# One GpSimd copy of 4096 columns for each landed pair of weight units, in place of two of 2048, in a hybrid attention and mixture-of-experts block

## What is computed

```python
logits = (xt @ router_w + router_b)
top_v, top_e = lax.top_k(logits, TOP_K)          # 4 of 32 experts for each of 256 tokens
wts = jax.nn.softmax(top_v, axis=-1)
...
hgu = xb @ w_gate_up[e] + b_gate_up[e]           # 1024 x 2048 for each expert
gate, up = jnp.split(hgu, 2, axis=-1)
gate = jnp.minimum(gate, SWIGLU_LIMIT)
up = jnp.clip(up, -SWIGLU_LIMIT, SWIGLU_LIMIT)
act = (up + 1.0) * (gate * jax.nn.sigmoid(SWIGLU_ALPHA * gate))
return act @ w_down[e] + b_down[e]               # 1024 x 1024 for each expert
```

## Time and profile before

| what | us or share |
|---|---|
| median of three runs | 1407.03 |
| the profiled execution's own time | 1406.08 |
| its span, first to last instruction | 1404.4 |
| TensorE (PE) busy | 1348.0, 96% of the span |
| GpSimd (POOL) busy | 709.1, 50% |
| VectorE (DVE) busy | 399.0, 28% |
| ScalarE (ACT) busy | 236.9, 17% |
| landing transfers | 186 of 2048 KB, median 10.7 us from issue to landing |
| mean granted clock of TensorE | 0.988 of 2.4 GHz |

### The profile page before, as it was taken

How to read it: one execution, slowest core, us unless ns; L and a number is a source line. 1 busy time by engine, 2 the same in 40 slices (tenths; PEclk the granted TensorE clock), 3 DMA queues, 4 the chain that set the end, 5 groups by cost and what they waited for, 6 DMA issues and landing times.

```text
span 1404.4 us, 17038 instructions
## 1 busy us (share of the span) xinstructions
PE 1348.0 (96%) x6424; PEld 619.6 (44%) x6425; DVE 399.0 (28%) x751; ACT 236.9 (17%) x404; POOL 709.1 (50%) x413
## 2 busy tenths in 40 slices
PE   5999999999989999999999999999999999899996
PEld 2888445888643333333333333333333332233332
DVE  2150014565664213322232231123322211111112
ACT  2320024210022111111211211111211211111112
POOL 0000000000015427777587777777777777777774
PEclk9999999999979999999999999999999999999998
DMA  9743533599678658999799999999999999999995
GB/s 351 256 166 120 176 123 120 197 349 364 220 270 342 246 249 336 427 429 429 321 429 429 428 428 429 427 403 429 429 429 428 428 427 429 429 427 429 428 429 231
DMA packets 70913, 485.87 MB, mean 346 GB/s; under 512 B 7254, under 2 KB 7418, under 8 KB 45450
## 3 DMA queue, kind: packets, MB, share of 16 engines
q1 hardware_dynamic: 69490, 480.56, 83.5%
q0 software_dynamic: 1056, 3.93, 1.0%
q10 hardware_dynamic: 344, 1.07, 0.2%
HBM read 483.44 MB, written 2.10 MB: 346 GB/s over the span
## 4 chain that ended last, share of the span: by engine, by line
PE 50%; DMA 44%; POOL 1%; issue 1%; DVE 1%; SPq 1%; ACT 1%; POOLq 0%; DVEq 0%; ACTq 0%
DMA landing<-in_w_gate_up 29%; PE bank L1195 15%; DMA landing<-in_w_down 14%; PE bank L1531 12%; PE bank L1569 6%; PE bank L1204 6%; PE bank L1497 2%; PE bank L1430 2%; DMA piece<-in_w_ada 1%; PE bank L1545 1%; POOL dn_slot L503 1%; SPq L379 1%; PE bank L1559 0%; PE bank L1473 0%; PE bank L1409 0%
## 5 line engine op out<-in xcount | busy, mean ns | idle before, releaser
L503 POOL COPY gu_slot<-landing 128x2048 f32<-128x2048 f32 x248 | 462.9, 1896 | 208.3 <-issue 116.6
L1531 PE MATMUL bank<-gu_slot,xg 128*64 128x512 f32 x2304 | 518.8, 596 | 24.4 <-POOL gu_slot L503 24.2
L1531 PEld LDWEIGHTS bank<-gu_slot,xg 128*64 128x64 f32 x2304 | 159.5, 137 | 356.9 <-issue 273.4
L503 POOL COPY dn_slot<-landing 128x2048 f32<-128x2048 f32 x124 | 231.1, 1894 | 76.5 <-issue 56.5
L1569 PE MATMUL bank<-dn_slot,actT 128*64 128x512 f32 x1152 | 255.1, 595 | 0.0
L1569 PEld LDWEIGHTS bank<-dn_slot,actT 128*64 128x64 f32 x1152 | 79.5, 137 | 171.2 <-issue 171.2
L1195 PE MATMUL bank<-hT,piece 128*128 128x256 f32 x704 | 153.4, 380 | 0.0
L1126 DVE TENSOR_SCALAR bank<-bank 128x512 f32<-128x512 f32 x36 | 25.2, 700 | 417.7 <-PE bank L1531 417.7
L719 ACT ACTIVATE sig<-bank 128x512 f32<-128x512 f32 x36 | 21.5, 597 | 724.7 <-PE bank L1531 724.7
L1195 PEld LDWEIGHTS bank<-hT,piece 128*128 128x128 f32 x704 | 133.5, 190 | 19.0 <-issue 1.1
L1135 DVE TENSOR_TENSOR ysb<-bank,gt2q 128x512 f32<-128x512 f32 x36 | 24.9, 692 | 265.6 <-PE bank L1569 265.6
(11 more groups left out here) (292 smaller groups left out, 904.1 us busy)
## 6 DMA issues: line engine op xcount, KB each, us to landing
landing<-in_w_gate_up SPq DMA_DIRECT2D x124, 2048.0 KB, 10.7
landing<-in_w_down SPq DMA_DIRECT2D x62, 2048.0 KB, 10.7
piece<-in_w_in SPq DMA_DIRECT2D x17, 2048.0 KB, 8.6
piece<-in_w_ada SPq DMA_DIRECT2D x12, 2048.0 KB, 13.0
gu_slot<-in_w_gate_up SPq DMA_DIRECT2D x8, 1024.0 KB, 7.2
piece<-in_w_branch_a SPq DMA_DIRECT2D x2, 2048.0 KB, 9.2
dn_slot<-in_w_down SPq DMA_DIRECT2D x4, 1024.0 KB, 11.2
piece<-in_w_branch_b SPq DMA_DIRECT2D x2, 2048.0 KB, 8.5
```

Of the source, the lines that this page charges most:

```text
L503: nc.gpsimd.tensor_copy(place, landing[j // 2 % 3][:, j % 2, :]).then_inc(there, 16)
L1531: ins = M(gu_bank[u][64 * q:64 * q + 64, :], xg[:, k % 4, 64 * (k // 4):64 * (k // 4) + 64], gu_slot[k][:, cols_], start=(k == 0), stop=(k ...
```

## The change

Two units that lay side by side become one pair, with one tensor for both; gu_slot and dn_slot stay as views of its halves. GpSimd copies a landed block as one instruction of 4096 columns. It waits for the block's landing and for both units to have been used, and its end raises only the second unit's semaphore (gu_in or dn_in of 1, 3, 5, 7). TensorE waits once for each pair: for the second unit's semaphore at the value of the body's expert, and for the first unit's at 16, which the direct load of expert 0 brings it to. SyncE's waits stay as they are. VectorE's wait near the end is moved from gu_in[0] to gu_in[1].

```diff
-        gu_slot = [sb(f"gu_slot{j}", 8 * j, [P, 2048]) for j in range(8)]
-        dn_slot = [sb(f"dn_slot{j}", 64 + 8 * j, [P, 2, D]) for j in range(4)]
+        gu_pair = [sb(f"gu_pair{j}", 16 * j, [P, 4096]) for j in range(4)]
+        dn_pair = [sb(f"dn_pair{j}", 64 + 16 * j, [P, 4096]) for j in range(2)]
+        gu_slot = [gu_pair[j // 2][:, 2048 * (j % 2):2048 * (j % 2) + 2048] for j in range(8)]
+        dn_slot = [dn_pair[j // 2][:, 2048 * (j % 2):2048 * (j % 2) + 2048].rearrange("p (r n) -> p r n", r=2) for j in range(4)]
...
-                for j in range(12):
-                    place, there, used = ((gu_slot[j][:], gu_in[j], gu_used[j]) if j < 8 else
-                                          (dn_slot[j - 8][:].rearrange("p r n -> p (r n)"), dn_in[j - 8], (dn_used + [y_full])[j - 8]))
-                    pool.wait_ge(unit_landed[j // 2], 16 * e)
-                    pool.wait_ge(used, free)
-                    nc.gpsimd.tensor_copy(place, landing[j // 2 % 3][:, j % 2, :]).then_inc(there, 16)
+                for n in range(6):
+                    if n < 4:
+                        first, second, place, there = gu_used[2 * n], gu_used[2 * n + 1], gu_pair[n], gu_in[2 * n + 1]
+                    else:
+                        i = 2 * (n - 4)
+                        first, second, place, there = (dn_used + [y_full])[i], (dn_used + [y_full])[i + 1], dn_pair[n - 4], dn_in[i + 1]
+                    pool.wait_ge(unit_landed[n], 16 * e)
+                    pool.wait_ge(first, free)
+                    pool.wait_ge(second, free)
+                    nc.gpsimd.tensor_copy(place[:], landing[n % 3][:].rearrange("p a n -> p (a n)")).then_inc(there, 16)
...
-            dve.wait_ge(gu_in[0], 16 * E)
+            dve.wait_ge(gu_in[1], 16 * E)
...
-                    pe.wait_ge(gu_in[k], landed)
+                    if k % 2 == 0:
+                        pe.wait_ge(gu_in[k], 16)
+                        pe.wait_ge(gu_in[k + 1], landed)
...
-                    if f % 2 == 0:
-                        pe.wait_ge(dn_in[f // 2], landed)
+                    if f % 4 == 0:
+                        pe.wait_ge(dn_in[f // 2], 16)
+                        pe.wait_ge(dn_in[f // 2 + 1], landed)
```

## The result

| kernel | median of its runs, us | lowest to highest | ratio, 95% interval |
|---|---|---|---|
| before (5 runs) | 1406.84 | 1405.56 to 1408.17 | |
| changed (5 runs) | 1413.85 | 1413.80 to 1416.22 | 1.0045 [1.0032, 1.0057] |

The changed kernel is slower by 7.0 us. The forecast was 1414.2 us, made of a sum of 7.2 us at four places. The profiled execution took 1414.0 us by its own time, with a span of 1412.3 us.

The account below looks back on a forecast made before the run. The end was taken to be set by a path alternating between DMA and TensorE; 1.83 + 1.77 + 1.83 + 1.77 = 7.2 us on 1407.03 gave 1414.2 us, range 1410.4 to 1417.5.

Parts of the forecast that it names:

- four places: Where the limiting path changes hands between DMA and TensorE, at 684, 903, 921 and 1374 us; together 7.2 us.
- C: Time of one joined 128x4096 GpSimd copy, taken as 3.67 us, the middle of 3.61 and 3.73.
- Places 1 and 3: DMA restarts at 684 and 921 us: the joined copy waits for both units to be used; 1.83 us each.
- Places 2 and 4: Handovers to TensorE at 903 and 1374 us: it waits for the whole last gate/up pair; 1.77 us each.
- Costed at nothing: Delays before 668 us, GpSimd's fewer waits and TensorE's paired waits: 0 us, covered by queued work or idle time.
- the lower bound of the two: TensorE's two waits on one instruction: 0 us from below, 2.9 us from above; 0 was taken.
- A loop bound by its own latency: Rival: the landing-buffer loop limits, not the DMA; shorter copies save 5.0 us, ending at +2.0 us; chance 0.06.
- Absorbed restarts: Rival: later DMA slack makes the restarts at 684 and 921 us free; +3.5 us, 1410.6; chance 0.10.
- The stop near 924 us: The DMA's second stop, under 2 us before, was to grow by 3.6 us.
- VectorE's blocked operations: Rival: small VectorE operations stand behind longer copies up to 3.7 us, making TensorE wait; 6 us more, 1420; chance 0.05.
- Medians unchanged: Expected profile: VectorE's median operation times stay as before while maxima rise to near 3.7 us.
- no more than the shift already there: After the 684 us restart, the down pair starts about 1.75 us later, covered by the existing delay; no added cost.

Follow-up runs that it names:

- e1: Kernel before, twelve copies kept, but TensorE waits for both units of a pair ahead of the first: 1411.20 us, ratio 1.0034.
- e2: Kernel before, twelve copies kept, but GpSimd's first copy of a pair waits until TensorE has used both units: 1411.56 us, ratio 1.0032.
- e3: Kernel before with both coarser waits, on TensorE and GpSimd, still twelve copies of 2048 columns for each expert: 1414.86 us, ratio 1.0057.
- e6: Changed kernel with the first and last gate/up pairs (0 and 3) copied again as two units with their own waits: 1414.32 us, ratio 1.0047.
- e8: Changed kernel with every pair split again except the first down pair, the only joined one left: 1410.89 us, ratio 1.0023.
- e7: Changed kernel with gate/up pairs 0, 1, 3 and the first down pair split again, two pairs left joined: 1410.77 us, ratio 1.0030.

## Why the prediction was right

**The bound and the four places.** The sum was 7.2 us, the loop shows 7.0 and the medians 7.0. The chance of 0.88 went to slower. That the coarse waits are the cause, each half at its two places, is shown by e1, e2 and e3.

**C.** I took 3.67 us between 3.61 and 3.79; it is 3.60. The extrapolation by columns was the better end, and it too was slightly high. It makes 0.07 us at each place.

**Places 1 and 3**: 1.83 forecast each, 1.84 and 1.83 measured. That they match in spite of the smaller C is luck, two small errors of opposite sign: the first transfer after the stop is issued at 690.94 us in place of 688.26, which is 1.71 us later when the shift of 0.97 is taken off, and the other 0.13 us arose in the DMA, where the landing events of a transfer lie 0.90 us apart in place of 0.78.

**Places 2 and 4**: 1.77 forecast each, 1.68 and 1.61 measured. TensorE starts 1.80 us later at place 2 (908.23 less 903.62 is 4.61, less the shift of 2.81), which is C - 1.90 and a longer gap between the end of the copy and the matmul: 0.14 us (908.09 to 908.23) in place of 0.04. But its 16 matmuls then take 3.65 us in place of 3.77, since it doesn't wait for the second unit; that 0.12 us the working left out.

**Costed at nothing.** The body that TensorE holds takes 25.92 us (475.70 to 501.62 in the chain of waits), as before. So where data are there, the paired waits cost nothing, the lower bound of the two. The step of 4.89 us holds.

**The rivals.** A loop bound by its own latency would have shortened the step: it is 4.89, at shares of 1.01. Absorbed restarts would have left places 1 and 3 near 0: the second restart is issued at 931.47 us in place of 925.28 (the last issue of four that end at 925.61), 5.2 later when the shift of 0.97 is taken off, and the point below which this rival would have held was 5. The stop near 924 us grew by 3.4 us, forecast 3.6. VectorE's blocked operations doubled in length at most, and TensorE never waited for them.

**Wrong in detail.** "Medians unchanged" for VectorE failed: iota's median is 2545 ns, because TensorE's coarse waits moved the bodies against the copies (e1 and e3), which the working left out. And one step was right only in its surroundings: "no more than the shift already there", said of the down pair at 703.09 us. In the changed kernel that holds. But it was argued from the delay of the first pair, and so it made the loss look as if it hung on pairs 0 and 3, and e6, built on that, came out 7 us over its forecast. The down pair alone costs 1.5 to 1.9 us at each restart (e8). So the four places are right as a sum for this change, and wrong as a list of the pairs that may be joined.

**What stays open.** Why the 2 to 6 us in which the DMA runs low show 262 to 328 GB/s at shares of 0.68 to 0.97, and why the landing events of a transfer lie further apart from then on, isn't settled. Nor is why one wait of 2.92 us left TensorE's clock as it was and five did not.

## What to carry to other kernels

A join of two copies joins their waits as well: price it where the path changes hands, as the length of the part that used to go first, and not by the instructions saved on an engine with idle time. Costs of coarse waits in one chain don't add: undoing one may give nothing, or make it worse, until the next is undone, so a first-order attribution needs the experiment with one coarse wait alone. A last stage that needs no double buffering can skip the staging copy, but only once the copy that then stands last is off the path too: six direct units gained nothing that the times could show, eight gained 2 us.

## What was not expected of the hardware

- TensorE's clock: around 906 us in e7, after a wait of 2.92 us, the granted clock was 0.82 from 908 to 915 us, and 32 matmuls took 8.78 us in place of 7.09. Five of six such waits had this, one did not; after waits of up to 1.76 us the 32 took 7.09.
- DMA: after a transfer issued 1.5 us late, or a buffer freed 1.7 us late, the 16 landing events of every transfer up to the next stop lay up to 3.2 us apart in place of 0.78 (e6), and the last of them is what the copy waits for.
- DMA: 1 MB transfers with 8 KB in each partition ran at 422 GB/s where 2 MB transfers with 16 KB ran at 428 to 429, both at a share of 1.01; a packet took 313 and 613 ns.
- GpSimd: copies of 4096 columns take 3.60 us, and back to back start 3.55 us apart ((10.69 - 3.60) / 2); VectorE's iota, 0.20 us by itself, is held by a copy in 25 of 33 bodies (up to 3583 ns), where the kernel before held it in 16 of 33 (up to 1849 ns).
